# Output projection in two parts, the first between the attention heads; two heads begun among the input tiles

## The reference

```python
def token_mixer(h, ...):
    proj = h @ w_in                              # 1024 -> 2312: z, xbc, dt, xp, q, k, v
    xbc = silu(causal_depthwise_conv(xbc)); y_ssd = gated, group-normed ssd_chunked(...)   # width 512
    y_pool = multiscale_pool(xp, pool_w, pool_scale)                                       # width 256
    y_sb = stick_breaking_attention(q, k, v)     # 4 heads of 64: z = q.k/8 (causal)
    return concatenate([y_ssd, y_pool, y_sb]) @ w_out

def block(q_blk, i):                             # of the attention
    log_beta = log_sigmoid(z); log_keep = where(mask, log_beta - z, 0.0)
    later = cumsum(log_keep, reverse=True) - log_keep
    w = where(mask, exp(log_beta + later), 0.0)
    return w @ v

def reference(x, c, ...):
    for l in range(2):
        sh1, sc1, g1, sh2, sc2, g2 = split(silu(c) @ ada_w[l] + ada_b[l], 6)
        x = x + g1 * token_mixer(modulate(rms_norm(x), sh1, sc1), ...)
        x = x + g2 * peer_ffn(modulate(rms_norm(x), sh2, sc2), ...)
    return rms_norm(x)
```

## Time and profile before

| | |
|---|---|
| median of 3 runs | 3204.47 us (3200.95 to 3204.57) |
| profiled execution | 3206.76 us, span 3205.0 us |
| TensorE busy, mean granted clock | 3063.0 us (96%), 0.981 |
| VectorE (DVE) busy | 2443.5 us (76%) |
| ScalarE (ACT) busy | 1510.2 us (47%) |
| GpSimd (POOL) busy | 839.6 us (26%) |
| chain that ended last | PE 88% of the span; L836 (`project`) 45%, L1232 (expert v tiles) 30% |

### The profile page before, as it was taken

How to read it: one execution, slowest core, us unless ns; L and a number is a source line. 1 busy time by engine, 2 the same in 40 slices (tenths; PEclk the granted TensorE clock), 3 DMA queues, 4 the chain that set the end, 5 groups by cost and what they waited for, 6 DMA issues and landing times.

```text
span 3205.0 us, 47747 instructions
## 1 busy us (share of the span) xinstructions
PE 3063.0 (96%) x17460; PEld 2848.0 (89%) x17460; DVE 2443.5 (76%) x4276; ACT 1510.2 (47%) x2394; POOL 839.6 (26%) x655
## 2 busy tenths in 40 slices
PE   6988899999999999999989789999999999999998
PEld 3755679999999999999978468999999999999997
DVE  5564689888886688878876648996888857888787
ACT  3343224478886333333352532345888733333333
POOL 1000005644443222222200000464444422222221
PEclk8989999999999999999999899999999999999999
DMA  6523445689999999999922012467999999999996
GB/s 239 183 74 151 165 177 174 201 288 369 357 345 375 341 358 345 340 349 347 349 103 73 14 66 86 135 207 244 337 364 367 338 357 326 347 346 348 346 346 218
DMA packets 261680, 840.83 MB, mean 262 GB/s; under 512 B 23856, under 2 KB 73264, under 8 KB 248880
## 3 DMA queue, kind: packets, MB, share of 16 engines
q1 hardware_dynamic: 174000, 470.28, 41.6%
q0 software_dynamic: 80640, 318.80, 26.9%
q10 hardware_dynamic: 6912, 50.33, 3.7%
HBM read 736.56 MB, written 102.76 MB: 262 GB/s over the span
## 4 chain that ended last, share of the span: by engine, by line
PE 88%; DVE 4%; DMA 4%; ACT 3%; issue 1%; POOL 0%; DVEq 0%; SPq 0%; ACTq 0%; POOLq 0%
PE bank L836 45%; PE bank L1232 30%; PE bank L1216 5%; DMA w_raw<-wst 2%; PE bank L852 2%; PE bank L890 1%; PE bank L1154 1%; DMA gate_matrices<-stage 1%; DMA ada_buf<-adaw 1%; ACT w_hi L592 1%; DVE w_lo L1274 1%; PE bank L985 0%; PE bank L1002 0%; DVE zs L1554 0%; DVE arg L1593 0%
## 5 line engine op out<-in xcount | busy, mean ns | idle before, releaser
L592 ACT ACTIVATE w_hi<-w_raw 128x1024 fp32r<-128x1024 f32 x596 | 631.5, 1060 | 989.3 <-PE bank L836 734.9
L1274 DVE TENSOR_TENSOR w_lo<-w_raw,w_hi 128x1024 fp32r<-128x1024 f32 x516 | 632.5, 1226 | 609.3 <-ACT w_hi L592 603.0
L836 PE MATMUL bank<-hH,w_hi 128*128 128x384 f32 (+1 forms) x2656 | 943.9, 355 | 16.6 <-DVE hL L1614 6.8
L836 PE MATMUL bank<-hH,w_lo 128*128 128x384 f32 (+1 forms) x2656 | 924.5, 348 | 0.0
L836 PE MATMUL bank<-hL,w_hi 128*128 128x384 f32 (+1 forms) x2656 | 924.1, 348 | 0.0
L1232 PE MATMUL bank<-c_hi,w_hi 128*128 128x384 f32 x2048 | 685.9, 335 | 6.3 <-ACT act_out L768 3.2
L1232 PE MATMUL bank<-c_hi,w_lo 128*128 128x384 f32 x2048 | 684.1, 334 | 0.0
L1232 PE MATMUL bank<-c_lo,w_hi 128*128 128x384 f32 x2048 | 684.1, 334 | 0.0
L836 PEld LDWEIGHTS bank<-hH,w_hi 128*128 128x128 f32 x2656 | 500.9, 189 | 68.6 <-issue 30.8
L836 PEld LDWEIGHTS bank<-hH,w_lo 128*128 128x128 f32 x2656 | 500.2, 188 | 24.9
L836 PEld LDWEIGHTS bank<-hL,w_hi 128*128 128x128 f32 x2656 | 501.2, 189 | 21.9
(11 more groups left out here) (259 smaller groups left out, 2725.1 us busy)
## 6 DMA issues: line engine op xcount, KB each, us to landing
w_raw<-wst SPq DMA_DIRECT2D x596, 512.0 KB
activations<-act_out SPq DMA_DIRECT2D x128, 384.0 KB
gate_matrices<-stage ACTq DMA_DIRECT2D x48, 1024.0 KB
act_in<-activations SPq DMA_DIRECT2D x64, 768.0 KB, 6.6
gates<-gate_matrices SPq DMA_DIRECT2D x64, 768.0 KB
ada_buf<-adaw POOLq DMA_DIRECT2D x32, 1024.0 KB, 6.6
nrm<-adaw POOLq DMA_DIRECT2D x8, 1024.0 KB, 5.1
pj<-adaw POOLq DMA_DIRECT2D x4, 1024.0 KB, 5.1
```

Of the source, the lines that this page charges most:

```text
L592: nc.scalar.activation(w_hi[g % 2][:, :, :].rearrange("p a b -> p (a b)"), w_raw[:, g % RAWS, :], ACT.Copy).then_inc(s_wh, 1)
L836: last = mm(bank[s][:, 0:t.stop - t.start], a[s][:, k, :], b[:, k, t], start=(k == 0 and a is w_hi and b is hH), stop=(k == KT - 1 and a i ...
L1274: v.tensor_tensor(w_lo[g % 2][:, :, :].rearrange("p a b -> p (a b)"), w_raw[:, g % RAWS, :], w_hi[g % 2][:, :, :].rearrange("p a b -> p (a ...
```

## The change

Five things change, all of them in the token mixer and the stage behind it.

1. The input tiles have another order: xs, B, C, xp 6-7, z 8-11, then q, k of heads 0-1 (12, 13), v (14, 15), q, k of heads 2-3 (16, 17). The weights are laid out to match. The pool's sums on DVE move from tiles 14-16 to 9-11, its mix on PE to after tile 12, the Silu of z to tile 12.
2. The scores of heads 0 and 1 are made in pieces after tiles 14, 15 and 16, in whatever PSUM halves are free (s_z counts 5 steps a layer now), and scaled by DVE at once. zs, ez, nlk and arg get places for more heads (on rows of `pj` that are used up).
3. ACT does Abs and Exp for two heads, then one table load, then both Lns (`att_exps`, `att_logs`); the copy of tile 17 stands behind them.
4. The output projection's weights are cut differently: 6 tiles hold the blocks of k 0-5 (48 blocks of 128x128, output part by output part), 2 tiles those of k 6-7 (16 blocks). `out_early(o)` adds k 0-5 of output part o and DVE adds the sum to x; `out_late(o)` does k 6-7 and DVE adds again, so x takes 16 additions instead of 8. The early parts begin when y and the pool's part are divided and heads 0 and 1 are out; sums and outputs of heads 2 and 3 stand between them.
5. The ada chunks of layer 1 stand in the query stage alone: two behind each of the first 9 query tiles, one behind the others. The norm's first group sums stand behind the last late part. The key load on SP waits for y instead of for the whole right side.

```diff
-XS0, B0, C0, Q0, K0, V0, XP0, Z0 = 0, 4, 5, 6, 8, 10, 12, 14
+XS0, B0, C0, XP0, Z0, Q0, K0, V0 = 0, 4, 5, 6, 8, 12, 13, 14
+PAIR = 4
+EARLY_K, LATE_K = 6, 2
+def chunks_of(n):
+    return [2 * n, 2 * n + 1] if n < 9 else [n + 9]
+ATT_BANK = (((2, 0), (3, 0), (4, 0), (3, 384)), ((5, 0), (6, 0), (7, 0), (6, 384)))
+ATT_OUT = (0, 1, 2, 5)
...
@@ SP
-                        sp.wait_ge(s_rhs, l * RHS_PARTS + KT + 1)
+                        sp.wait_ge(s_ymix, l + 1)
                         sp.dma_start(keys[:, :, :], keysT[l]).then_inc(s_keys, 16)
@@ ACT, after the tiles
+                att_exps(0)
+                att_exps(1)
+                nc.scalar.preload_act_table_set("natural_log")
+                att_logs(0)
+                att_logs(1)
+                root_table()
                 act.wait_ge(s_ygv, l * 4 + 4)
                 nc.scalar.activation(y_tok[:, :, :], xbc[:, 0:4, :], ACT.Square).then_inc(s_ysq, 1)
+                hi(l, OUT0 + 1)
+                tile_copy(N_IN - 1)
...
+                act.wait_ge(s_rhs, l * RHS_PARTS + KT + 1)
+                for k in range(KT - 1):
+                    act.wait_ge(s_taken, l * TAKEN + OUT0 + k + 3)
+                    norm_square(k)
+                    if k == 3:
+                        hi(l, WQ0)
@@ PE, among the tiles
+                    if n == 12:
+                        pool_mixed()
+                    if n == 14:
+                        pe.wait_ge(s_taken, l * TAKEN + K0 + 3)
+                        pe.wait_ge(s_seg, l * 8 + 8)
+                        score(0, 0, 6, 0)
+                        score(0, 1, 2, 0)
+                        score(0, 3, 2, 384).then_inc(s_z, 1)
...
@@ PE, after the tiles
+                def out_blocks(o, first, ks, t0):
+                    for k in range(len(ks)):
+                        b = o * len(ks) + k
+                        t, c = OUT0 + t0 + b // KT, b % KT
+                        if c == 0 or k == 0:
+                            pe.wait_ge(s_wh, l * STREAM + t + 1)
+                            pe.wait_ge(s_wl, l * STREAM + t + 1)
+                        for a, r in ((w_hi, hH), (w_hi, hL), (w_lo, hH)):
+                            last = mm(bank[o % 2][:, :], a[t % 2][:, c, :], r[:, ks[k], :], ...)
+                att_sums(0)
                 if l == 0:
                     pe.wait_ge(s_arow, ADA_SETS)
                     modulation(0, 1, 7)
                     modulation(0, 2, 7)
...                                                   # square sums of y
+                att_sums(1)
+                att_scores(2)
+                att_out(0)
+                att_scores(3)
+                att_out(1)
+                pe.wait_ge(s_mx, l + 1)
+                out_early(0)
+                out_early(1)
+                att_sums(2)
+                out_early(2)
+                att_sums(3)
+                out_early(3)
+                out_early(4)
+                att_out(2)
+                out_early(5)
+                att_out(3)
+                out_early(6)
+                out_early(7)
+                pe.wait_ge(s_rhs, l * RHS_PARTS + KT + 1)
+                for o in range(N_OUT):
+                    out_late(o)
+                norm_groups(2 * l + 1, 0)
                 norm_groups(2 * l + 1, 4)
@@ DVE, after the tiles
+                att_keep(0)
+                ...                                   # v copies
+                att_keep(1)
+                lo(l, OUT0 + 1)
+                ...                                   # modulation taken
+                att_arg(0)
+                mixed_low(1, 4, 6)
+                att_masked(0)
+                y_normed(0)
+                y_normed(1)
+                att_arg(1)
+                att_scaled(2)
+                att_taken(0)
+                mixed_low(2, 0, 4).then_inc(s_mx, 1)
+                att_masked(1)
+                att_scaled(3)
+                att_taken(1)
+                att_keep(2)
+                att_keep(3)
+                early_taken(0)
+                lo(l, OUT0 + 2)
+                early_taken(1)
+                mixed_low(3, 6, 7)
+                att_arg(2)
+                att_masked(2)
+                early_taken(2)
+                lo(l, OUT0 + 3)
+                att_arg(3)
+                att_masked(3)
+                early_taken(3)
+                lo(l, OUT0 + 4)
+                early_taken(4)
+                early_taken(5)
+                lo(l, OUT0 + 5)
+                att_taken(2)
+                att_taken(3)
+                mixed_low(4, 7, 8).then_inc(s_rhs, 1)
+                early_taken(6)
+                lo(l, OUT0 + 6)
+                early_taken(7)
+                lo(l, OUT0 + 7)
                 for k in range(N_OUT):
+                    late_taken(k)
+                    if k == 3:
+                        lo(l, WQ0)
```

More of the change, by code:

```diff
@@ L239, in build @@
         scan.close()
[L241 to L248, removed]
+        early = ExitStack()
+        sb("before_xdd", [P, 6 * T + 2 * NT * T], where=early)
+        arg = [sb("arg0", [P, WA], where=early)]
+        ez = [sb(f"ez{s}", [P, WA], where=early) for s in range(2)]
+        early.close()
+        sb("to_xdt", [P, 6 * T], where=mixer)
+        nlk = [sb("nlk0", [P, WA], where=mixer)]
+        mixer.close()
+        raw_rows = pj[:, 0:Z0, :].rearrange("p a t -> p (a t)")
+        arg.append(raw_rows[:, 0:WA])
+        zs += [raw_rows[:, WA:2 * WA], raw_rows[:, 2 * WA:3 * WA]]
+        nlk.append(pj[:, Z0:Z0 + 4, :].rearrange("p a t -> p (a t)")[:, 0:WA])
         mixer.close()
@@ L670, in _ @@
                     hi(l, n + 2)
-                    nc.scalar.activation(pj[:, n, PAD:PJW], bank[n % 2][:, :], ACT.Copy).then_inc(s_taken, 1)
+                    tile_copy(n)
                     if 1 <= n <= CONVS:
@@ L1117, in _ @@
-                att_scores(0)
+                def out_blocks(o, first, ks, t0):
[6 more added lines that the diff above has]
+                        for a, r in ((w_hi, hH), (w_hi, hL), (w_lo, hH)):
+                            last = mm(bank[o % 2][:, :], a[t % 2][:, c, :], r[:, ks[k], :],
+                                      start=(k == 0 and a is w_hi and r is hH),
+                                      stop=(k == len(ks) - 1 and a is w_lo))
+                        if c == KT - 1:
+                            last.then_inc(s_tile, 1)
+                        elif k == len(ks) - 1:
+                            last.then_inc(s_op, 1)
@@ new lines, in _ @@
+                pe.wait_ge(s_ydv, l * 4 + 4)
+                pe.wait_ge(s_zv, l * SCORES + 3)
+                for j in range(2):
+                    for tt in range(NT):
+                        last = nc.tensor.transpose(bank[5 + j][:, tt * P:(tt + 1) * P],
+                                                   pj[:, V0 + j, PAD + tt * P:PAD + (tt + 1) * P], ident[:, :])
+                last.then_inc(s_vt, 1)
+                att_sums(0)
+                if l == 0:
+                    pe.wait_ge(s_arow, ADA_SETS)
+                    modulation(0, 1, 7)
+                    modulation(0, 2, 7)
@@ new lines, in att_masked, with att_taken @@
+                def att_masked(h):
+                    w = arg[h % 2]
+                    dve.wait_ge(s_w, l * 4 + h + 1)
+                    for i in range(NT):
+                        ins = v.tensor_tensor(w[:, O4[i]:O4[i] + P], w[:, O4[i]:O4[i] + P], tri_lt[:, :], ALU.mult)
+                    ins.then_inc(s_wm, 1)
+                def att_taken(h):
+                    r = slice(64 * (h % 2), 64 * (h % 2) + 64)
+                    dve.wait_ge(s_ay, l * 4 + h + 1)
+                    v.tensor_copy(mixed[r, 6 + h // 2, :], bank[ATT_OUT[h]][r, :]).then_inc(s_ayv, 1)
```

384 lines of the change are left out of this document (207 added, 177 removed).

## The result

The kernel after takes 3153.06 us (median of 4 runs, 3146.57 to 3155.14), beside 3202.71 us (3200.26 to 3204.57) for the kernel before in the same comparison: ratio 0.9842, 95% interval 0.9825 to 0.9859. It is 49.7 us faster; forecast were 44.0 and a time of 3160. Repeated on other occasions the same kernel gave 0.9827 (0.9813 to 0.984) and 0.9802 (0.9786 to 0.9818), so the ratio itself moves by some 0.4% between comparisons, and the gain is 50 to 64 us.

A forecast was written before the change was run, and what follows sets the result against it. PE was taken as busy nearly throughout except in two serial attention chains. Savings of 32.0 and 37.2 less 13.6, 2 and 9.6 gave 44.0 us saved, so 3160 us; range 3141 to 3188 (forecast's own 3149 to 3173).

The forecast's parts named there:

- Until the early part: From the end of input tile 17 to the first early matmul, layer 1: 36.1 us, near 37 in the windows.
- hand-overs: Passing work between engines in the serial part: some 12 at 0.15 us, taking layer 1's stretch from 97.2 to 99.0.
- two table switches ahead of keep 0: ACT's table loads before head 0's log keep, one before tile 17's end; next instruction 1.30 us after each load's start.
- Sums 0: PE's sums of head 0 after an idle time: run slowly, 6.7 us, between 4.5 and 7.55.
- The early and the late part: Output projection with heads 2 and 3 inside, from 36.1 to 97.2 us; late part has 2.7 us of waits.
- What is paid elsewhere: Costs outside the stretches: pool mix and scores among input tiles 13.6, late pool segments 2, ada chunks 9.6 us.
- the ada chunks: Eight chunks of layer 1 moved into the full query stage of layer 0: 1.2 us each, 9.6 us.
- 1 (the queue of DVE or ACT bounds the projection): Early part: w_lo behind head work, 2.5 us at each of 6 tiles, two layers, 30 us lost: 3190; chance 0.18.
- 2 (the lower clock through the projection, slower than before): PE stays at 1.2 GHz through the projection, 38.4 us a layer, 77 in both: 3237, slower; chance 0.05.
- 3 (ada chunks late): Query stage: ada chunks come late, 2 us at each of 9 tiles, 18 us: 3178; chance 0.07.
- 4: PE holds full clock from head 0's sums on and hand-overs are covered: 10 us more saved, 3150; chance 0.10.
- The two rules: Skill rules against the rows: dearer table switches would make the saving 39 us; depth-cycling speaks against late part and interleaved heads.

The follow-up runs named there:

- e3: Kernel after with one table load and logarithm for each of heads 0 and 1 in turn, instead of both together; 3149.16 us, ratio 0.983.
- e6: Kernel after with two unused matmuls ahead of head 0's sums, in layer 1 alone; 3144.5 us, ratio 0.982.
- c_after2: Kernel after, unchanged, run once more in the third comparison; 3140.35 us, ratio 0.9802 to the kernel before.
- e5: Kernel after with two idle DVE operations ahead of the low part of weights of output tiles 2 to 6; 3146.5 us, ratio 0.983.
- e4: Kernel after with ACT's and DVE's weight copies for the first query tile in another order; 3145.64 us, ratio 0.9818.
- e9: Kernel after with four idle DVE operations ahead of the low part of weights of output tiles 2 to 6; 3172.06 us, ratio 0.99.
- e2: Kernel after with scores and scaling of heads 0 and 1 moved behind input tile 17; 3170.4 us, ratio 0.9899.
- c_after: Kernel after, unchanged, run again in the first comparison; 3147.72 us, ratio 0.9827 to the kernel before.

## Why the prediction was right, and where it was off

**What bounded the kernel.** Right, and by experiment: undoing the two ways in which PE gets other work during the serial chain costs 22.5 and 22.7 us, 44.4 together. The other 9.5 us of that comparison were not traced to a part of the change.

**Until the early part.** Foreseen 36.1 us after E plus hand-overs (37), measured 33.8 and 32.6. The step that was off is ACT's head 0: logarithm 0 was done at 0.8 instead of 2.9. The prediction counted two table switches ahead of keep 0, one of them before E; that one did not take place, since the set loaded at 1719.85 still served Exp, and it is 1.3 of the 2.1 us. The other 0.8 is ACT being ahead of the prediction's count, not traced further. So nlk 0 was there at 3.4 instead of 5.4, sums 0 ended at 9.5 instead of 12.2, sums 1 at 17.4 instead of 20.5, and the early part began 3.5 earlier. e3 shows how far that carries: more speed on ACT would win 0.6 us, since DVE is in y's gate until E + 0.3. Sums 0 were put at 6.7 us for both layers, and took 6.12 in layer 1 and 4.43 in layer 0; that DVE's chain hangs on them was right, and e6 and c_after2 show what it is worth.

**The early and the late part.** 61.1 us foreseen (36.1 to 97.2), 60.5 measured. No wait for w_lo, as forecast; spare times were put at 2 us and more, and e5, which takes 2.4 us of each, costs one wait of 1.05. The late part was to wait 2.7 us, in the takes behind w_lo of the query tile; it waited 0.48 + 1.80 = 2.3, and e4 shows that this is the place of the 1.80. The stretches, 100.6 and 99.0 foreseen, were 94.3 and 93.2: 6.3 and 5.8 less, some 3.5 of it before the early part and 1.8 the hand-overs, which I had added on top and which the sum did not need.

**What is paid elsewhere.** Forecast 13.6 + 2 + 9.6 = 25.2; measured 7.2 + 18.4 = 25.6. Inside that sum the ada chunks were sized too high: 7.1 us for 8 of them, 0.9 each instead of 1.2, with PE busy for 130.54 of 131.6 us, so no load was late. The input tiles of layer 1 took 10.4 more where 7.8 were forecast. Of it, pool mix 2.0, scores 4.8 and a wait of 0.8 for segments make 7.6; the other 2.7 is a lower clock at the head of that stage (0.97 over the stage, 0.99 before). The edit costs what was said, and the clock there comes on top in this execution. That the whole of what is paid came out within 0.4 us is therefore luck: the chunks were 2.5 too high, and this clock, 2.7, was not in the sum.

**The sum.** Foreseen 44.0, measured between medians 49.7, and 60.2 between the two profiled executions. 11.7 of the 16.2 between 44.0 and 60.2 are the stretches (81.3 for 69.2 foreseen, less 0.4 paid elsewhere); 4.4 are in the rest of layer 1, mostly in its expert stage, which the change does not touch (1185.6 to 1181.6 us) and which moves by as much between executions. That the profiled execution of after was the fastest of its four explains part of the distance to the medians. Why the whole kernel moved from 3153 to 3140 us between comparisons, while the kernel before stayed within 3 us, is open. The clock is part of it: the stretch of layer 0 was 94.3, 97.2 and 93.0 us in three executions of the same kernel, and in the second the projection had a clock of 0.96. That of layer 1 was 93.2, 93.2 and 91.5.

**The rivals.** 1 (the queue of DVE or ACT bounds the projection) is false here, and e5 and e9 show from where it would be true: between 12 and 24 us of added DVE work a layer. 2 (the lower clock through the projection, slower than before) is false: the clock was 1.00 in five of the six projections of the kernel after that were profiled, and 0.96 in the sixth. 3 (ada chunks late) is false: no wait for them in the query stage. 4 had two parts: hand-overs covered, which is what happened, and full clock from sums 0 on, which did not: the clock between E and the early part was 0.88 to 0.95 in those six. Its 3150 is nearer to 3153 than the forecast of 3160 is: of the chance of 0.10 that it had, too little stood on the hand-overs, which alone are 1.8 us a layer, and none on the table load that did not take place.

**The two rules.** A table load and the next instruction are again 1.29 us apart (1752.10, 1753.39). The Trainium skill, "ScalarE: Activation LUTs", section "What ACT_TABLE_LOAD costs", gives 2.66 us for a switch, a load of 1.28 us and a drain behind it. The load has that length here (1.28 us); the drain does not show between it and the next instruction. The projection has heads and bank changes in it and waits of 0.48 and 1.80, and its clock was 1.00 in after. The Trainium skill, "TensorE: Matmul & The Clock Gate", section "A second HAM failure mode: psum-queue depth-cycling", describes a loss through short idle times at bank changes, which this stretch does not have there. The 3.5 us that e9 lost lie behind a wait of 3.93 us for w_lo, which is another thing.

## What to carry to other kernels

Where a serial chain of small steps on other engines leaves TensorE idle, look for independent matmuls to put between its links, and for links that can be done among full tiles; both were worth 22 us here and they added. Count such a stretch engine by engine, in queue order: that sum came within 7% of each stretch. Test the cover by adding idle work to the engine that is said to have room, since a trace shows busy time and not how much more would fit. And before making one link of the chain earlier, follow what hangs on it to the end: in e3 the earlier logarithm made a copy late that the next link needed, and in e6 the faster sums brought output 1 forward by 1.6 us, which a lower clock took back.

## What was not expected of the hardware

- Waiting is paid twice where the clock falls behind it. In e9, with waits of 10.9 us a layer, PE's same matmuls took 3.5 us more, and in e2 3.8 us of waits were enough for eight transposes to take 1.94 us instead of 1.04.
- The same idle time did not always lower the clock. Behind 2.50 us of waiting, sums 0 of layer 1 took 6.12 us in one execution of the kernel after and 4.43 us in two others (c_after, c_after2), and output 1 behind them took 2.37 us in one of these two and 4.06 in the other.
- An activation table set stays in place over other functions: behind the load at 1719.85 ACT did exponentials, copies and Abs for 28 us, and Exp still ran 1.30 us after the start of Abs, with no load between. In the kernel before, where a Silu came between, a load stood there (1785.59).
